# Attention output projections: three contraction pairs in the third and fourth column blocks take seven block products, not eight, in both layers

## The chip, the cores and the metric

The kernel runs on one core of one Trainium2 chip. The metric is the device time of one execution in microseconds (us). TensorE is called PE, VectorE DVE, ScalarE ACT; SP is the engine that only issues DMAs here.

## The reference, cut to what matters

A two-layer trunk, 256 tokens, 2048 columns, float32. Layer 0 mixes tokens with forgetting attention (FoX, 16 heads of 128), layer 1 with sliding-window attention (SWA, 32 heads of 64). Each mixer ends in an output projection of shape 256x2048 by 2048x2048, and then comes a gated MLP.

```
def fox_mixer(...):
    ...
    return o.reshape(b, s, FOX_QKV) @ w_out      # 2048 x 2048
def swa_mixer(...):
    ...
    return o.reshape(b, s, SWA_Q) @ w_out        # 2048 x 2048
for i in range(DEPTH):
    h = rms_norm(x, attn_norm[i]); x = x + mixer(h, ...)
    h = rms_norm(x, ffn_norm[i]);  x = x + conv_glu_ffn(h, ...)
```

## The kernel before, in words

**Numbers in two parts.** Every float32 operand of a large product is split into a high part (rounded to fp32r) and a low part (the rest). A product is three matmuls: high by high, low by high, high by low. For weights, ACT copies `raw` to `whi` and DVE subtracts to get `wlo`; both happen for every unit.

**Units.** Weights stream in units of 128 x 1024 floats (512 KB), through four slots (`RAW = 4`) of `raw`, `whi`, `wlo`. SP loads unit u when `wlo` of unit u-4 is made. In the list of steps that every engine follows in the same order, the step `("unit", u, ...)` means: PE multiplies unit u; ACT and DVE convert unit u+4 (`conv_hi`, `conv_lo`). ACT can begin that conversion only when PE has finished unit u, since the slot is the same.

**The output projection.** It has 32 units, numbered 0 to 31 here. A unit is one column block g (512 of the 2048 output columns) and two of the 16 contraction tiles (j, 0 to 7). It takes 12 matmuls of 128 x 512: 2 contraction tiles x 2 token tiles x 3. The activations are `oT` (high and low). Blocks are walked g = 0, 1, 2, 3 with all j each (FoX), or 0 and 1 interleaved, then 2, then 3 (SWA).

**The border into the MLP.** When block g is complete, DVE adds it to the residual stream `xk` (`res`, `residual`, L1052). One unit later PE transposes those columns (`xt`, L1484, 8 transposes), and ACT and DVE scale them into `hs` (`prep`, L732 and L1060, four instructions each); ACT also squares them (`ss`, L723). `transposes(n, g)` waits for `res` of its own block and, for g above 0, for `prep` of the block before:

```
pe.wait_ge(v_x, x_after(n, g))
pe.wait_ge(v_hl, KT * n + 4 * g - (4 if g == 0 else 0))
```

**The down projection of the MLP** already has units of another kind, in pairs "s" and "t". Such a pair covers two column blocks and the same contraction rows as two plain units, with seven products of blocks (Strassen-Winograd) in place of eight. For it DVE first makes sums of weight blocks (`seven_sums`, L1007, L1009, L1011, into `tsum`), ACT and DVE split the sums (`thi` L698, `tlo` L989, 128x2048), and after the last pair the products are combined into `xk` in two parts (`seven_out`, L1020 to L1031; step `ev`). The activation sums for it (`xs`) were made earlier and come back from memory.

Of the kernel before, what the change touches and what calls it, by code (L numbers as in the profile page):

```python
# [29 lines left out]
P = 128  # L30
# [75 lines left out]
PAIRS = [(layer, c, i) for layer, order in enumerate(DOWN_ORDER) for i, (kind, c, k) in enumerate(order) if kind == "s"]  # L106
# [22 lines left out]
def trunk(nc, x, attn_norm, ffn_norm, fox_w_in, fox_f_bias, fox_q_norm, fox_k_norm, fox_w_out,  # L129
# [7 lines left out]
    with ExitStack() as ctx:  # L137
# [62 lines left out]

        qT = rg("qT", [P, 4, T])
# [45 lines left out]
        nsk = rg("nsk", [P, SWA_GROUPS, 2])  # L247
        gq = sb("gq", [P, SWA_D])
# [115 lines left out]
        a_ev = sem("a_ev")  # L364
        v_e = sem("v_e")
# [26 lines left out]
        def fox_plan():  # L392
            steps = []
            for p in range(FOX_GROUPS + 1):
# [22 lines left out]
                for i in range(24 if p < FOX_GROUPS else OUT_EARLY):  # L417
                    if p < FOX_GROUPS:
                        steps += front.get(i, [])
                        steps.append(("unit", fox_unit(24 * p + i), "QKV"[i // 8], p, i % 8))  # L420
                        steps += new.get(i, [])
                    else:
                        steps.append(("unit", U_FOX_OUT + i, "o", 0, i))
                    if p == 0:
                        steps += first.get(i, [])
                    else:
                        steps += old.get(i, [])
            return steps

        def swa_plan():  # L430

            steps = []
            for slot in range(8 * SWA_CHUNKS + SWA_OUT_EARLY):
# [18 lines left out]
                if slot < 8 * SWA_CHUNKS:  # L452
                    steps.append(("unit", U_SWA + slot, "W", slot // 8, slot % 8))
                else:
                    n = slot - 8 * SWA_CHUNKS
                    steps.append(("unit", U_SWA_OUT + n, "o") + SWA_ORDER[n])
# [4 lines left out]
        def border_steps(units, n, last):  # L461

            steps, waiting = [], None
            for u, kind, g, j in units:
# [11 lines left out]
        def out_plan(base, first, n):  # L476
            order = FOX_ORDER if n == 1 else SWA_ORDER
            return border_steps([(base + i, "o") + order[i] for i in range(first, OUT_UNITS)], n, 7)
# [26 lines left out]
        def seven_kind(u):  # L505

            for m, (layer, c, i) in enumerate(PAIRS):
                if u - down_unit(layer, i) in (0, 1):
                    return "st"[u - down_unit(layer, i)], m
            return None, None  # L510

        def pairs_done(layer, c):

            return sum(p[:2] <= (layer, c) for p in PAIRS)

# [40 lines left out]
        def xt_banks(n, g):  # L556

            return (4, 6, 2, 4)[g] if n == 0 else 4
# [23 lines left out]
        def _(sp):  # L582
# [43 lines left out]
            for n in range(OUT_UNITS):  # L626
                load(U_FOX_OUT + n, rows(fox_w_out[0], 2 * (n % 8), 2, 512 * (n // 8), 512), (U_FOX_OUT + n) % RAW)

            def ffn_loads(layer):
# [14 lines left out]
                for i, (kind, g, k) in enumerate(DOWN_ORDER[layer]):  # L644
                    col = {"d": g, "s": 2 * g, "t": 2 * g + 1}[kind]
                    load(down_unit(layer, i), rows(ffn_w_down[layer], 2 * k, 2, 512 * col, 512), down_unit(layer, i) % RAW)
                    kind, m = seven_kind(down_unit(layer, i) - 2)
                    if kind == "s":
                        if first_pair(m):
                            sp.wait_ge(unit_done, down_unit(layer, 0))  # L650
                            sp.wait_ge(v_glo, UP_GROUPS * (layer + 1) + 1)
                            sp.wait_ge(x_sent, 16 * (MIX_GROUPS * (layer + 1) + 1))
                        if m >= RING:
                            sp.wait_ge(unit_done, down_unit(PAIRS[m - RING][0], PAIRS[m - RING][2]) + 2)
                        group = DOWN_ORDER[layer][PAIRS[m][2]][2] // 2
                        sp.dma_start(xs[m % RING][:, :, :, :].bitcast(F32).rearrange("p a h t -> p (a h t)"), mix[layer, group + 1, :, :])\
                            .then_inc(x_back[m % RING], 16)
# [7 lines left out]
            for n, (g, j) in enumerate(SWA_ORDER):  # L665
                load(U_SWA_OUT + n, rows(swa_w_out[0], 2 * j, 2, 512 * g, 512), (U_SWA_OUT + n) % RAW)
# [14 lines left out]
        def _(act):  # L681
# [5 lines left out]
            def conv_hi(u, slot):  # L687
# [5 lines left out]
                if kind == "t":  # L693
                    act.activation(whi[slot][:, 0:512], raw[slot][:, 0:512], ACT.Copy).then_inc(hi_ready, 1)
                    act.wait_ge(v_t, 3 * m + 3)
                    if m:
                        act.wait_ge(v_tl, m)
                    act.activation(thi[:, :, :], tsum[:, :, :], ACT.Copy).then_inc(a_th, 1)  # L698
# [10 lines left out]
            def square_x(n, g):  # L709
# [10 lines left out]
                if n == 2:  # L720
                    act.wait_ge(v_e, 7 * 2)
# [21 lines left out]
            def step(s):  # L743
# [10 lines left out]
                elif kind == "ev":  # L754
                    if s[3] == 0:
                        act.wait_ge(unit_done, s[4] + 1)
                        act.wait_ge(v_tl, pairs_done(n // 2 - 1, s[2]))
                        act.activation(tsum[:, 0, :], ps[:, 6, :], ACT.Copy).then_inc(a_ev, 1)
# [212 lines left out]
        def _(dve):  # L971
            tt = dve.tensor_tensor

            def conv_lo(u):
# [10 lines left out]
                if kind == "t":  # L985
# [3 lines left out]
                    tt(tlo[:, :, :], tsum[:, :, :], thi[:, :, :].bitcast(F32), ALU.subtract).then_inc(v_tl, 1)  # L989
# [3 lines left out]
            def seven_sums(u, m):  # L993

                layer, c, _ = PAIRS[m]
# [4 lines left out]
                if first_pair(m):  # L1000
# [3 lines left out]
                if m:  # L1004
                    dve.wait_ge(v_tl, m)
                    dve.wait_ge(v_e, 7 * (2 * layer + c))
                tt(tsum[:, 0:2, :], both[:, 1:3, :], b12, ALU.add).then_inc(v_t, 1)  # L1007
                dve.wait_ge(v_t, 3 * m + 1)
                tt(tsum[:, 2, :], tsum[:, 0, :], b22, ALU.add).then_inc(v_t, 1)  # L1009
                dve.wait_ge(v_t, 3 * m + 2)  # L1010
                tt(tsum[:, 3, :], tsum[:, 2, :], b21, ALU.add).then_inc(v_t, 1)  # L1011

            def seven_out(n, c, part, u):

                e0, q = 7 * (2 * (n // 2 - 1) + c), lambda b: ps[:, b, :]
# [24 lines left out]
            def residual(n, g, u):  # L1040
# [3 lines left out]
                if n % 2 == 0:  # L1044
                    dve.wait_ge(v_e, 7 * (2 * (n // 2 - 1) + g // 2 + 1))
# [18 lines left out]
            def step(s):  # L1064
# [266 lines left out]
        def _(pe):  # L1331
# [16 lines left out]
            def seven_unit(s):  # L1348

                _, u, kind, c, k = s  # L1350
                layer, i = (0 if u < U_SWA else 1), k // 2
                m, slot = seven_kind(u)[1], u % RAW
                first, last = i == 0, i == SEVEN[layer][c] - 1
                w = lambda buf, kj: buf[slot][:, 512 * kj:512 * kj + 512]
                sums = lambda buf, a: buf[:, a, :]
                act_in = lambda f, t: (lambda h: gs[:, i, f, h, t * P:t * P + P])
                mixed = lambda a: (lambda h: xs[m % RING][:, a, h, :])
# [8 lines left out]
                if kind == "s":  # L1366
                    if first:
                        pe.wait_ge(v_up, UP_GROUPS * (layer + 1) + 1)
                        if c:
                            pe.wait_ge(v_e, 7 * (2 * layer + c))  # L1370
                    product(4, act_in(1, 0), w(whi, 1), w(wlo, 1), first, last)
                    product(0, act_in(0, 0), w(whi, 0), w(wlo, 0), False, False).then_inc(unit_done, 1)
# [5 lines left out]
                product(5, mixed(3), sums(thi, 0), sums(tlo, 0), first, last)  # L1378
                product(7, mixed(1), sums(thi, 1), sums(tlo, 1), first, last)
                product(6, mixed(0), sums(thi, 2), sums(tlo, 2), first, last)  # L1380
                product(1, act_in(0, 1), sums(thi, 3), sums(tlo, 3), False, False).then_inc(unit_done, 1)

            def token_unit(s):
# [7 lines left out]
                opens = at == FIRST_OF[layer][g] if kind == "d" else j == 0  # L1391
# [77 lines left out]
            def transposes(n, g):  # L1469

                if n:
                    pe.wait_ge(v_x, x_after(n, g))
                    pe.wait_ge(v_hl, KT * n + 4 * g - (4 if g == 0 else 0))
                    if n == 2 and g == 0:
                        pe.wait_ge(v_up, UP_GROUPS + 1)
                        pe.wait_ge(v_e, 7 * 2)
# [223 lines left out]
```

## Time and profile before

| | |
|---|---|
| time, median of 3 runs | 2081.77 us (2080.77 to 2082.47) |
| the profiled execution: its own time | 2082.18 us |
| its span, first to last instruction | 2080.4 us |
| PE busy | 2072.3 us, 10836 matmuls |
| DVE busy | 1472.2 us |
| ACT busy | 1069.1 us |

The span is what the trace covers; about 1.8 us of the execution's time lie outside it. Matmul ends are modelled, so distances between matmuls are read from start to start. A time that an engine sat idle, and what ended it, stands in brackets at the end of a timeline row.

### The profile page before, as it was taken

How to read it: one execution, taken by the hardware profiler on the slowest of the kernel's cores; microseconds unless marked ns; L12 is line 12 of the kernel's file. 1: busy time of each engine (PE TensorE's matmuls, PEld its weight loads, DVE VectorE, ACT ScalarE, POOL GpSimd, SP SyncE). 2: the span in 40 equal slices, each digit the busy share in tenths (PEclk: the TensorE clock that was granted, in tenths of full speed). 3: DMA queues.
4: the chain of work that ended last, by engine and by line, in shares of the span. 5: the costliest groups of instructions: out<-in, count | busy, mean ns of one | idle time of the engine just before them, and what ended most of it. 6: DMA issues, size and time to landing. Idle time of an engine off the chain costs nothing.

```text
span 2080.4 us, 30179 instructions
## 1 busy us (share of the span) xinstructions
PE 2072.3 (100%) x10836; PEld 1772.4 (85%) x10836; DVE 1472.2 (71%) x1794; ACT 1069.1 (51%) x1379; POOL 0.7 (0%) x5
## 2 busy tenths in 40 slices
PE   9999999999999999999999999999999999999999
PEld 8888888888888888888888888888888888888887
DVE  5655565567767767778886687566767767778987
ACT  6545555554444544455555566554444444455553
POOL 0000000000000000000000000000000000000000
PEclk9999999999999999999999999999999999999999
DMA  7655555656666566578786544566656666668786
GB/s 251 213 172 173 168 173 179 187 174 208 195 202 204 191 200 212 192 226 258 242 254 185 181 149 139 173 189 192 193 192 220 191 196 209 200 206 260 244 258 208
DMA packets 214043, 419.02 MB, mean 201 GB/s; under 512 B 13724, under 2 KB 18636, under 8 KB 213964
## 3 DMA queue, kind: packets, MB, share of 16 engines
q1 hardware_dynamic: 211660, 415.76, 63.5%
q10 hardware_dynamic: 2304, 2.20, 0.3%
q8 instruction: 50, 0.82, 0.2%
q14 instruction: 29, 0.24, 0.0%
HBM read 405.31 MB, written 12.60 MB: 201 GB/s over the span
## 4 chain that ended last, share of the span: by engine, by line
PE 95%; DVE 3%; ACT 1%; issue 1%; DMA 1%; DVEq 0%; ACTq 0%
PE ps L1345 37%; PE ps L1335 31%; PE ps L1341 16%; PE ps L1360 2%; PE ps L1362 2%; PE ps L1361 2%; PE ps L1484 1%; DVE wlo L991 0%; DMA raw<-in_ffn_w_down 0%; PE ps L1541 0%; PE ps L1553 0%; PE ps L1570 0%; PE ps L1587 0%; PE ps L1606 0%; PE ps L1596 0%
## 5 line engine op out<-in xcount | busy, mean ns | idle before, releaser
L1335 PE MATMUL ps<-hs,whi 128*128 128x512 f32 x2832 | 663.6, 390 | 0.0
L1335 PEld LDWEIGHTS ps<-hs,whi 128*128 128x128 f32 x2832 | 524.7, 188 | 104.3
L1038 DVE TENSOR_TENSOR wlo<-raw,whi 128x1024 fp32r<-128x1024 f32 x352 | 418.1, 1222 | 254.8 <-PE ps L1341 222.8
L991 DVE TENSOR_TENSOR wlo<-raw,whi 128x1024 fp32r<-128x1024 f32 x342 | 413.7, 1222 | 215.1 <-ACT whi L700 214.6
L700 ACT ACTIVATE whi<-raw 128x1024 fp32r<-128x1024 f32 x344 | 363.2, 1059 | 341.3 <-PE ps L1345 281.0
L707 ACT ACTIVATE whi<-raw 128x1024 fp32r<-128x1024 f32 x352 | 366.0, 1056 | 265.5 <-DMA raw<-in_ffn_w_up 206.2
L1341 PEld LDWEIGHTS ps<-hs,wlo 128*128 128x128 f32 x2816 | 352.6, 191 | 8.8
L1341 PE MATMUL ps<-hs,wlo 128*128 128x256 f32 x2816 | 355.3, 283 | 0.0
L1345 PE MATMUL ps<-whi,hs 128*128 128x512 f32 x1088 | 273.9, 394 | 0.7 <-ACT whi L700 0.7
L1345 PEld LDWEIGHTS ps<-whi,hs 128*128 128x128 f32 x1088 | 201.4, 188 | 41.9 <-DVE hs L1060 0.9
L1345 PE MATMUL ps<-whi,gs 128*128 128x512 f32 x864 | 214.2, 389 | 0.0
L1345 PEld LDWEIGHTS ps<-whi,gs 128*128 128x128 f32 x864 | 161.9, 188 | 33.4
L1345 PE MATMUL ps<-wlo,hs 128*128 128x512 f32 x544 | 145.7, 389 | 0.0
L1345 PE MATMUL ps<-whi,oT 128*128 128x512 f32 x512 | 128.6, 393 | 0.6 <-DVE oT L1232 0.6
L1345 PEld LDWEIGHTS ps<-wlo,hs 128*128 128x128 f32 x544 | 102.1, 188 | 21.4
L1345 PE MATMUL ps<-wlo,gs 128*128 128x512 f32 x432 | 116.0, 389 | 0.0
L1345 PEld LDWEIGHTS ps<-whi,oT 128*128 128x128 f32 x512 | 94.8, 188 | 20.7 <-DVE oT L1232 0.8
L1345 PEld LDWEIGHTS ps<-wlo,gs 128*128 128x128 f32 x432 | 81.1, 188 | 16.8
L698 ACT ACTIVATE thi<-tsum 128x2048 fp32r<-128x2048 f32 x34 | 65.2, 1919 | 43.8 <-DVE tsum L1011 43.8
L989 DVE TENSOR_TENSOR tlo<-tsum,thi 128x2048 fp32r<-128x2048 f32 x34 | 78.0, 2293 | 8.8 <-ACT thi L698 8.8
L1277 DVE SCALAR_TENSOR_TENSOR ybuf<-gbuf,conv,ybuf 128x256 f32<-128x256 f32 x176 | 73.5, 481 | 0.0
L935 ACT ACTIVATE gs<-hf 128x1024 f32 (+1 forms) x22 | 23.3, 1061 | 91.7 <-DVE hf L1288 91.7
(190 smaller groups left out, 1558.5 us busy)
## 6 DMA issues: line engine op xcount, KB each, us to landing
raw<-in_ffn_w_up SPq DMA_DIRECT2D x352, 512.0 KB, 4.1
raw<-in_ffn_w_down SPq DMA_DIRECT2D x176, 512.0 KB, 5.4
raw<-in_fox_w_in SPq DMA_DIRECT2D x98, 512.0 KB, 4.1
raw<-in_swa_w_in SPq DMA_DIRECT2D x40, 512.0 KB, 3.7
xs<-mix SPq DMA_DIRECT2D x34, 512.0 KB, 6.4
raw<-in_fox_w_out SPq DMA_DIRECT2D x32, 512.0 KB, 4.6
raw<-in_swa_w_out SPq DMA_DIRECT2D x32, 512.0 KB, 3.9
mix<-mix_out SPq DMA_DIRECT2D x20, 512.0 KB, 6.2
```

The lines of the kernel that those rows point to most:

```text
L698: act.activation(thi[:, :, :], tsum[:, :, :], ACT.Copy).then_inc(a_th, 1)
L700: act.activation(whi[slot][:, :], raw[slot][:, :], ACT.Copy).then_inc(hi_ready, 1)
L707: act.activation(whi[u0 % RAW][:, :], raw[u0 % RAW][:, :], ACT.Copy).then_inc(hi_ready, 1)
L989: tt(tlo[:, :, :], tsum[:, :, :], thi[:, :, :].bitcast(F32), ALU.subtract).then_inc(v_tl, 1)
L991: tt(wlo[slot][:, :], raw[slot][:, :], whi[slot][:, :].bitcast(F32), ALU.subtract).then_inc(lo_ready, 1)
L1038: tt(wlo[slot][:, :], raw[slot][:, :], whi[slot][:, :].bitcast(F32), ALU.subtract).then_inc(lo_ready, 1)
L1277: last = dve.scalar_tensor_tensor(ybuf[:, f, :], gbuf[:, f, w:w + T], c(w), ybuf[:, f, :], ALU.mult, ALU.add)
L1335: return pe.matmul(ps[:, bank, :], whi[slot][:, c:c + P], moving.rearrange("p h t -> p (h t)"), start=first, stop=last)
L1341: return pe.matmul(ps[:, bank, 0:T], wlo[slot][:, c:c + P], moving[:, 0, :], start=False, stop=last)
L1345: return pe.matmul(ps[:, bank + t, :], src[:, h, t * P:(t + 1) * P], w[slot][:, 512 * kj:512 * kj + 512], start=first, stop=last)
L1360: pe.matmul(ps[:, bank, :], x(0), hi, start=start, stop=False)
L1361: pe.matmul(ps[:, bank, :], x(1), hi, start=False, stop=False)
```

## The change

In both output projections, three pairs of units of blocks 2 and 3 (j = 0, 2, 4) become pairs "s" and "t" of seven products. The other five j of these blocks stay plain. The order of the units changes: (2,1), (3,1), then s0 t0, (2,3), (3,3), s2 t2, (2,5), (3,5), s4 t4, then (2,6), (2,7), (3,6), (3,7), as (g, j). Blocks 0 and 1 stay as they are. The products use buffers of their own, `tsum_o`, `thi_o`, `tlo_o`; the activation sums are made by DVE and ACT from `oT`, in steps `xf`, `xc`, `xs` after units 5, 7 and 9. The transposes of block 1 go to another bank.

```
 def out_order(n):
...
+    plain(OUT_LEAD[n])
+    for s, j in enumerate(seven_j):
+        order.extend((("s", 1, j), ("t", 1, j)))
+        if s < OUT_SEVEN[n] - 1:
+            plain(1)
+    order.extend([("o", g, j) for g in (2, 3) for j in left])
...
+        SUMS = {1: {5: "xf", 7: "xc", 9: "xs"}, 3: {5: "xf", 7: "xc", 9: "xs"}}
...
+                u, (kind, g, j) = base + i, OUT_ORDER[n][i]
+                if i - LAST_OUT_SEVEN[n] in (1, 2):
+                    steps.append(("ev", n, 1, i - LAST_OUT_SEVEN[n] - 1, base + LAST_OUT_SEVEN[n]))
                 if j == last:
                     steps.append(("res", n, g, u))
                 steps.append(("unit", u, kind, g, j))
-                if n <= 3 and waiting is not None:
+                if waiting is not None:
                     steps += [("xt", n, waiting), ("prep", n, waiting)]
                     waiting = None
-                if n <= 3 and j == last:
+                if j == last:
                     steps.append(("ss", n, g))
                     waiting = g
+                if i in SUMS[n]:
+                    steps.append((SUMS[n][i], n))
...
         def xt_banks(n, g):
 
+            if n % 2 and g == 1:
+                return 2 if n == 1 else 0
             return (4, 6, 2, 4)[g] if n == 0 else 4
...
+                elif kind == "xs":
+                    act.wait_ge(o_xc, n // 2 + 1)
+                    act.activation(xs_o[n][:, :, :, 0, :], xc_o[n][:, :, :, :], ACT.Copy).then_inc(o_xh, 1)
...
+                elif kind == "xf":
+                    dve.wait_ge(*((v_ol, FOX_H) if n == 1 else (s_ol, 2 * OUT_SEVEN[n] - 1)))
...
+                    tt(xf_o[n][:, :, :, :], part(0), part(1), ALU.add).then_inc(o_xf, 1)
+                elif kind == "xc":
...
+                    tt(s1, a21, a22, ALU.subtract)
+                    tt(s3, a11, a21, ALU.subtract).then_inc(o_x1, 1)
...
+                    tt(n1, a11, s1, ALU.subtract).then_inc(o_x2, 1)
...
+                    tt(s4, a12, n1, ALU.subtract).then_inc(o_xc, 1)
+                elif kind == "xs":
+                    dve.wait_ge(o_xh, n // 2 + 1)
+                    tt(xs_o[n][:, :, :, 1, :], xc_o[n][:, :, :, :], xs_o[n][:, :, :, 0, :].bitcast(F32), ALU.subtract).then_inc(o_xs, 1)
...
-                pe.wait_ge(x_back[m % RING], 16 * (m // RING + 1))
-                product(2, mixed(2), w(whi, 0), w(wlo, 0), False, False)
+                if n % 2:
+                    pe.wait_ge(o_xs, n // 2 + 1)
+                else:
+                    pe.wait_ge(x_back[RING_NO[m] % RING], 16 * (RING_NO[m] // RING + 1))
+                product(c2, mixed(2), w(whi, 0), w(wlo, 0), False, False)
```

**DVE where blocks 0 and 1 of SWA end (units 14, 15, 16).** L1052 is `res`, L991 `conv_lo`, L1060 `prep`. Before:

```order
L1052 TENSOR_TENSOR xk<-xk,ps 128x2x512 [waits unit_done]
L991 TENSOR_TENSOR wlo_55<-raw,whi_51 128x1024 [waits hi_ready]
L1052 TENSOR_TENSOR xk<-xk,ps 128x2x512 [waits unit_done]
L991 TENSOR_TENSOR wlo_56<-raw,whi_52 128x1024 [waits hi_ready]
L1060 SCALAR_TENSOR_TENSOR hs<-ps,gains,hs 128x256 [waits a_hh]
```

In the changed kernel L1131 is `res`, L1085 to L1089 make the weight sums, L1066 and L1061 are `conv_lo`, L1064 is the low part of the sums, L1139 is `prep`:

```order
L1131 TENSOR_TENSOR xk<-xk,ps 128x2x512 [waits unit_done]
L1085 TENSOR_TENSOR tsum_o<-raw 128x1024 [waits s_ol,v_tl,w_land1,v_e,w_land0,hi_ready]
L1087 TENSOR_TENSOR tsum_o<-tsum_o,raw 128x512 [waits v_t]
L1089 TENSOR_TENSOR tsum_o<-tsum_o,raw 128x512 [waits v_t]
L1066 TENSOR_TENSOR wlo_55<-raw,whi_51 128x1024
L1131 TENSOR_TENSOR xk<-xk,ps 128x2x512 [waits unit_done]
L1061 TENSOR_TENSOR wlo_56<-raw,whi_52 128x512 [waits hi_ready]
L1064 TENSOR_TENSOR tlo_o<-tsum_o,thi_o 128x2048 [waits a_th]
L1139 SCALAR_TENSOR_TENSOR hs<-ps,gains,hs 128x256 [waits a_hh]
```

Three sums now stand between the two residual additions, and the low part of the sums between the second one and `prep` of block 0. In FoX the same instructions stand around `res` of block 1 (there `prep` of block 0 is long done).

**DVE behind the last pair (units 27 to 30), the same in both layers.** Before, `res` of block 2 stood behind unit 23, with plain conversions on both sides:

```order
L991 TENSOR_TENSOR wlo_55<-raw,whi_51 128x1024 [waits hi_ready]
L1052 TENSOR_TENSOR xk<-xk,ps 128x2x512 [waits unit_done]
L991 TENSOR_TENSOR wlo_56<-raw,whi_52 128x1024 [waits hi_ready]
L991 TENSOR_TENSOR wlo_57<-raw,whi_53 128x1024 [waits hi_ready]
L1060 SCALAR_TENSOR_TENSOR hs<-ps,gains,hs 128x256 [waits a_hh]
```

In the changed kernel (L1099 to L1110 combine the products):

```order
L1066 TENSOR_TENSOR wlo_56<-raw,whi_52 128x1024 [waits hi_ready]
L1099 TENSOR_TENSOR tsum_o<-tsum_o,ps 128x512 [waits a_ev,unit_done]
L1100 TENSOR_TENSOR xk<-xk,ps 128x512
L1102 TENSOR_TENSOR tsum_o<-tsum_o,ps 128x512 [waits v_e]
L1103 TENSOR_TENSOR xk<-xk,ps 128x512
L1066 TENSOR_TENSOR wlo_57<-raw,whi_53 128x1024 [waits hi_ready]
L1106 TENSOR_TENSOR xk<-xk,tsum_o 128x2x512 [waits v_e]
L1108 TENSOR_TENSOR xk<-xk,tsum_o 128x512 [waits v_e]
L1110 TENSOR_TENSOR xk<-xk,ps 128x512 [waits v_e]
L1131 TENSOR_TENSOR xk<-xk,ps 128x2x512 [waits unit_done,v_e]
```

The residual addition of block 2 now stands behind all seven combining instructions. PE's transposes of block 2 still come after one further unit, now unit 30, and wait for it.

## Rows read from the trace of the kernel before

**Rows 1.** The page: busy us by engine; granted PE clock in 40 slices.

```profile
PE 2072.3 (100%) x10836; PEld 1772.4 (85%) x10836; DVE 1472.2 (71%) x1794; ACT 1069.1 (51%) x1379; POOL 0.7 (0%) x5
...
PEclk9999999999999999999999999999999999999999
```

**Rows 2.** Who waited for whom, PE: us in total, times, longest us.

```profile
PE ps L1664 <- DVE ones_t L1302: 1.2, 1, 1.2
PE ps L1360 <- DVE tlo L989: 1.0, 2, 0.8
```

**Rows 3.** Timeline: two plain units following each other (start us, us, instruction).

```profile
1350.16 1.98 PE L1345 MATMUL ps<-whi,oT 128*128 128x512 f32 x8
...
1352.88 1.98 PE L1345 MATMUL ps<-whi,oT 128*128 128x512 f32 x8
```

**Rows 4.** Timeline, down projection: a plain unit behind each of two pairs.

```profile
1033.92 1.98 PE L1345 MATMUL ps<-whi,gs 128*128 128x512 f32 x8
...
1044.12 1.98 PE L1345 MATMUL ps<-whi,gs 128*128 128x512 f32 x8
```

**Rows 5.** Groups by line: busy us, mean ns of one, idle before.

```profile
L991 DVE TENSOR_TENSOR wlo<-raw,whi 128x1024 fp32r<-128x1024 f32 x342 | 413.7, 1222 | 215.1 <-ACT whi L700 214.6
L700 ACT ACTIVATE whi<-raw 128x1024 fp32r<-128x1024 f32 x344 | 363.2, 1059 | 341.3 <-PE ps L1345 281.0 <-DMA raw<-in_ffn_w_down 44.4 <-PE ps L1362 9.8
L989 DVE TENSOR_TENSOR tlo<-tsum,thi 128x2048 fp32r<-128x2048 f32 x34 | 78.0, 2293 | 8.8 <-ACT thi L698 8.8
L698 ACT ACTIVATE thi<-tsum 128x2048 fp32r<-128x2048 f32 x34 | 65.2, 1919 | 43.8 <-DVE tsum L1011 43.8
L1011 DVE TENSOR_TENSOR tsum<-tsum,raw 128x512 f32<-128x512 f32 x34 | 23.5, 693 | 1.2
L1206 DVE TENSOR_TENSOR oT<-ps,oT 128x256 fp32r<-128x256 f32 x16 | 6.0, 416 | 0.0
```

**Rows 6.** Timeline, FoX, units 14 to 16.

```profile
355.41 1.23 DVE L991 TENSOR_TENSOR wlo<-raw,whi 128x1024 fp32r<-128x1024 f32 x1 [1.50 <-ACT whi L700]
...
356.98 1.22 DVE L1052 TENSOR_TENSOR xk<-xk,ps 128x1024 f32<-128x1024 f32 x1 [0.34 <-PE ps L1345]
...
359.51 1.03 PE L1484 MATMUL ps<-ident,xk 128*128 128x128 f32 x8
```

**Rows 7.** Timeline, SWA, units 14 to 16.

```profile
1310.01 1.23 DVE L991 TENSOR_TENSOR wlo<-raw,whi 128x1024 fp32r<-128x1024 f32 x1
...
1312.18 2.09 PE L1345 MATMUL ps<-whi,oT 128*128 128x512 f32 x8
...
1313.88 1.65 DVE L1060 SCALAR_TENSOR_TENSOR hs<-ps,gains,hs 128x256 fp32r<-128x256 f32 x4
...
1315.68 1.06 PE L1484 MATMUL ps<-ident,xk 128*128 128x128 f32 x8 [0.49 <-DVE hs L1060]
```

**Rows 8.** Timeline, down projection of layer 0: behind the last pair.

```profile
1084.92 1.98 PE L1345 MATMUL ps<-whi,gs 128*128 128x512 f32 x8
...
1093.51 1.07 PE L1484 MATMUL ps<-ident,xk 128*128 128x128 f32 x8 [0.27 <-DVE xk L1031]
```

**Rows 9.** Timeline, SWA: the last attention groups, beside units 7 to 11.

```profile
1285.37 1.23 DVE L991 TENSOR_TENSOR wlo<-raw,whi 128x1024 fp32r<-128x1024 f32 x1 [0.75 <-ACT whi L700]
...
1289.24 1.22 DVE L1215 TENSOR_REDUCE mxs<-ps 128x8 f32<-128x1024 f32 x1
...
1295.55 0.69 DVE L1229 TENSOR_TENSOR prs<-prs,rls 128x512 f32<-128x512 f32 x1
...
1298.35 1.04 PE L1596 MATMUL ps<-ident,prs 128*128 128x128 f32 x8
```

**Rows 10.** Issues of loads: KB each, median us from issue to landing.

```profile
raw<-in_swa_w_out SPq DMA_DIRECT2D x32, 512.0 KB, 3.9
```

**Rows 11.** Timeline: the first matmuls of the kernel, and the same shape later.

```profile
1.19 4.92 PE L1664 MATMUL ps<-ones_t 128*128 128x128 f32 x22 [1.19 <-DVE ones_t L1302]
...
7.41 1.06 PE L1672 MATMUL ps<-ones_t 128*128 128x128 f32 x8
```

More of the change, by code:

```diff
@@ L247, in trunk @@
         nsk = rg("nsk", [P, SWA_GROUPS, 2])
+        assert inr[0] <= xs_at
         gq = sb("gq", [P, SWA_D])
@@ L422, in fox_plan @@
                     else:
-                        steps.append(("unit", U_FOX_OUT + i, "o", 0, i))
+                        steps.append(("unit", U_FOX_OUT + i) + OUT_ORDER[1][i])
                     if p == 0:
@@ L459, in swa_plan, with out_plan @@
             return steps
-        def border_steps(units, n, last):
-            steps, waiting = [], None
-            for u, kind, g, j in units:
+        def out_plan(base, first, n):
+            steps, waiting, last = [], None, 7
+            for i in range(first, OUT_UNITS):
+                u, (kind, g, j) = base + i, OUT_ORDER[n][i]
+                if i - LAST_OUT_SEVEN[n] in (1, 2):
+                    steps.append(("ev", n, 1, i - LAST_OUT_SEVEN[n] - 1, base + LAST_OUT_SEVEN[n]))
                 if j == last:
@@ L505, in seven_kind, with seven_buffers, seven_banks, evicted @@
         def seven_kind(u):
-            for m, (layer, c, i) in enumerate(PAIRS):
-                if u - down_unit(layer, i) in (0, 1):
-                    return "st"[u - down_unit(layer, i)], m
+            for m, p in enumerate(PAIRS):
+                if u - p[2] in (0, 1):
+                    return "st"[u - p[2]], m
             return None, None
-        def pairs_done(layer, c):
-            return sum(p[:2] <= (layer, c) for p in PAIRS)
+        def seven_buffers(n):
+            return (tsum_o, thi_o, tlo_o) if n % 2 else (tsum, thi, tlo)
+        def seven_banks(n):
+            return {1: (0, 6, 4, 5, 2, 3), 3: (2, 6, 4, 5, 0, 1)}.get(n, (0, 2, 4, 5, 6, 7))
+        def evicted(n, c):
+            return 7 * STAGES.index((n, c))
+        def pairs_done(n, c):
+            return sum(p[:2] <= (n, c) for p in PAIRS)
         def first_pair(m):
@@ L697, in conv_hi @@
                         act.wait_ge(v_tl, m)
-                    act.activation(thi[:, :, :], tsum[:, :, :], ACT.Copy).then_inc(a_th, 1)
+                    act.activation(high[:, :, :], sums[:, :, :], ACT.Copy).then_inc(a_th, 1)
                     return
@@ L988, in conv_lo @@
                     dve.wait_ge(a_th, m + 1)
-                    tt(tlo[:, :, :], tsum[:, :, :], thi[:, :, :].bitcast(F32), ALU.subtract).then_inc(v_tl, 1)
+                    sums, high, low = seven_buffers(PAIRS[m][0])
+                    tt(low[:, :, :], sums[:, :, :], high[:, :, :].bitcast(F32), ALU.subtract).then_inc(v_tl, 1)
                     return
@@ L1366, in seven_unit @@
                 if kind == "s":
-                    if first:
+                    if first and n % 2:
+                        pe.wait_ge(v_hl, KT * n + 4)
+                    elif first:
                         pe.wait_ge(v_up, UP_GROUPS * (layer + 1) + 1)
                         if c:
-                            pe.wait_ge(v_e, 7 * (2 * layer + c))
-                    product(4, act_in(1, 0), w(whi, 1), w(wlo, 1), first, last)
-                    product(0, act_in(0, 0), w(whi, 0), w(wlo, 0), False, False).then_inc(unit_done, 1)
+                            pe.wait_ge(v_e, evicted(n, c))
+                    product(q1, act_in(1, 0), w(whi, 1), w(wlo, 1), first, last)
+                    product(c1, act_in(0, 0), w(whi, 0), w(wlo, 0), False, False).then_inc(unit_done, 1)
                     return
-                pe.wait_ge(x_back[m % RING], 16 * (m // RING + 1))
-                product(2, mixed(2), w(whi, 0), w(wlo, 0), False, False)
+                if n % 2:
+                    pe.wait_ge(o_xs, n // 2 + 1)
+                else:
+                    pe.wait_ge(x_back[RING_NO[m] % RING], 16 * (RING_NO[m] // RING + 1))
+                product(c2, mixed(2), w(whi, 0), w(wlo, 0), False, False)
                 pe.wait_ge(a_th, m + 1)
                 pe.wait_ge(v_tl, m + 1)
[L1378 to L1381, printed above, removed]
+                product(q5, mixed(3), sums(high, 0), sums(low, 0), first, last)
+                if first and n % 2:
+                    pe.wait_ge(v_hl, KT * n + 8)
+                product(q7, mixed(1), sums(high, 1), sums(low, 1), first, last)
+                product(q6, mixed(0), sums(high, 2), sums(low, 2), first, last)
+                product(c1 + 1, act_in(0, 1), sums(high, 3), sums(low, 3), False, False).then_inc(unit_done, 1)
             def token_unit(s):
```

130 lines of the change are left out of this document (88 added, 42 removed).

## The prediction

> **What bounds the kernel now.** I read the page first: PE is busy for 2072.3 of the 2080.4 us of the span, and its clock row shows nine tenths or more in every slice [rows 1]. Then the waits of PE: beyond the start there are none over 0.8 us [rows 2]. So the kernel is a stream of matmuls, and what I look for is how many matmuls go, and where PE will wait for DVE or ACT, which have had room until now. A plain unit takes 2.72 us from start to start, 0.227 us for each of its 12 matmuls [rows 3]. The rest of the reading was timelines of PE, DVE and ACT around the four places where the edit puts work: the end of attention in SWA, the border between blocks 1 and 2 in each layer, and the stretch behind the last pair in each layer. I followed the three engines' orders there, with durations from the rows.
>
> **What goes.** A pair has 21 matmuls where two plain units have 24. Three pairs in two layers take away 6 x 3 = 18 matmuls, all on the path: 18 x 0.227 = **-4.1 us**. That pairs run at the full rate of PE is seen in the down projection: a plain unit, a plain unit and a pair, 45 matmuls, take 10.20 us, 0.227 each [rows 4]. DVE has some 9.3 us to do in that time (two sums of 512, one of 1024, one `tlo`, three conversions and a half one: 2 x 0.69 + 1.22 + 2.29 + 3 x 1.22 + 0.69 [rows 5]), so it keeps up, barely. The Trainium skill, "TensorE: Matmul & The Clock Gate", section "Back-to-back issue gap", gives N/2.4 + 2.5 ns, 216 ns for 512 columns; by that figure the saving would be 3.9 us and the sum 0.2 us higher. The trace has 227 ns, and I take that.
>
> **What comes, first place: the border of blocks 0, 1 and 2 in FoX, +1.0 us.** The conversion of unit 18 (the first "s") happens at unit 14 and now has three sums ahead of it, 1.22 + 0.69 + 0.69 = 2.6 us [rows 5]. It began at 355.41; its `wlo` will then start at 358.0 and end at 359.2. Behind it in DVE's queue stands `res` of block 1, 1.2 us, so it ends at 360.4 and not at 358.2. PE's transposes of block 1, which began at 359.51 [rows 6], follow it by 0.15 us (the distance between `prep`'s end at 1313.88 + 1.65 and 1315.68 in [rows 7]): 360.5. PE waits 1.0 us. Next in the queue are `tlo` (to 363) and `prep` of block 1 (to 366.0); PE needs them at the second and third product of t0, 366.1 and 366.7. That fits, with 0.7 us to spare for the later one. Bounds: 0.5 (the sums overlap more) to 1.5 (that spare fails).
>
> **Second place: the same border in SWA, +3.9 us.** Here `prep` of block 0 comes behind the pair's work too. From 1310.01 [rows 7], as before but with sums: `wlo` of unit 18 ends at 1313.8, `res` of block 1 at 1315.0, the half conversion of unit 19 at 1315.7, `tlo` (2.29) at 1317.9, `prep` of block 0 (1.65) at 1319.5. ACT isn't the later one: `thi` can start at 1312.7 and ends at 1314.6, its half of `prep` at 1316.2. The transposes of block 1 wait for `prep` of block 0 (the second wait in `transposes`): they start at 1319.6, not at 1315.68. That is +3.9 us. PE could have started them at 1315.0 (1312.18 + 2.72, and 0.1 more for a unit that follows transposes: 2.09 there, 1.98 in [rows 3]), so it already lost 0.65 there. Behind that, `prep` of block 1 ends near 1322.6, and t0 needs it at 1325.8: covered. Bounds: 3.0 (all DVE steps overlap by 0.15 us) to 4.5.
>
> **Third place: the end of attention in SWA, +0.8 us.** Steps xf, xc and xs are new, and no row has their shapes. xf and the second half of xs have 1536 elements per partition: between 1.22 us (1024) and 2.29 (2048), 1.76 by line. ACT's copy of 1536 lies between 1.06 and 1.92: 1.49. xc is four operations of 384, between 0.42 and 0.69 each: 0.55, together 2.2 [rows 5]. xf stands ahead of a maximum of scores, and so delays ACT's exponentials and the conversion of unit 11 behind them by 1.7 less the idle 0.75: it ends at 1287.5. xc makes it 1289.7, the next conversion 1290.8, and the next maximum starts there and not at 1289.24 [rows 9]. ACT's exponentials follow 1.5 us late, then ACT's copy of xs puts 1.4 more ahead of the last group's, and DVE's half of xs 0.3 more ahead of its normalisation: `prs`, which ended at 1295.55 + 0.69 = 1296.2, ends at 1299.4. Its four transposes are the second half of the eight from 1298.35 [rows 9], due at 1298.75; they start at 1299.55. PE waits 0.8 us. With the smaller neighbours (1024, 256) it is 0; with the larger ones (2048, 512) 2.2. In FoX the same steps stand beside plain units, where DVE idles 1.5 us in each (the bracket in [rows 6]): nothing, and if that cover were gone, the 0.8 of here.
>
> **Fourth place: behind the last pair, +1.75 us in each layer.** The down projection shows this stretch: from the first unit behind the last pair, at 1084.92, to the transposes that waited for the last combining instruction, at 1093.51, are 8.59 us; three units are 8.16, so it cost only 0.27 there [rows 8]. In the projections `res` of block 2 stands between the last combining instruction and the transposes: +1.22 us. They can start 9.8 us after the last pair, where PE is ready at 8.16: a wait of 1.65. ACT's squares of block 2, `prep` of block 2 and `res` of block 3 shift with it; I get 0.1 us more at the transposes of block 3. Before, the transposes of block 2 had no such wait. Together **+3.5 us**. Bounds for each: 0.3 (as the down projection) to 2.3.
>
> **Loads.** SP's loads wait for `wlo` of four units earlier, so a late DVE issues them late. At the worst, behind the second place, unit 24 is loaded from 1320.6 and needed at 1330; a landing takes 3.9 us [rows 10]. Hidden. Without that cover it would be the excess over 9 us.
>
> **Sum**: -4.1 + 1.0 + 3.9 + 0.8 + 3.5 = **+5.1 us**. The profiled execution's own time is 2082.18, of which 2080.4 are the span; that is 0.4 above the median of the three runs. On the median, 2081.77 + 5.1 = **2086.9 us**, 0.25% slower. All low bounds give -4.1 + 0.5 + 3.0 + 0 + 0.6 = 0.0, all high ones +8.7.
>
> **The rivals.** (a) The waits don't come: DVE is busy for 71% only [rows 1], and 34 pairs in the down projections cost PE 1.0 us of waits in all [rows 2]. Then the 18 matmuls are the whole effect: 2077.7, faster by 0.2%. It decides if DVE is ahead by more than 4 us at 1310 and 2 us behind the last pairs; against it, `res` of blocks 0 and 2 can't start before PE's unit is done, so no lead can be stored up. (b) Only the end is shorter: the transposes of block 2 wait 0.3 us as in [rows 8]. Then 2086.9 - 2 x 1.4 = 2084.1. Against it stands the order, with `res` behind the last combining instruction. (c) The pairs don't catch up behind a late first one: DVE has 0.9 us of room in 10.2, and the second pair of the down projection waited 0.8 us [rows 2]. Once in each layer: +1.6, 2088.5. For it speaks the small room, against it that the second pair has 5.4 us of plain units ahead. (d) The clock. In SWA PE would stand still for 4.6 us before the transposes of block 1, longer than any wait of the trace. After its idle start, 22 matmuls of 128 columns took 4.92 us, 0.21 each; the same shape later takes 0.11 [rows 11], though the clock row shows no fall. Should PE restart like that, it would run at half its pace for some 5 us and lose 2.5: 2089.4. The Trainium skill, "TensorE: Matmul & The Clock Gate", section "Why this matters for your kernels", says that a long idle gap between bursts of matmuls brings PE back to half its clock; by that rule (d) is what happens, and the trace has no gap that tests it.
>
> **How the numbers follow.** 0.2% is 4.2 us, about what a measurement of this kernel can tell from no change. My forecast has a chance of 0.55, with its own range 2085.5 to 2088.3; 0.07 of it is below 2085.9, so within 0.2%. (a) 0.08, half of it faster by over 0.2%. (b) 0.12, within. (c) 0.10 and (d) 0.15, slower. Slower: 0.48 + 0.10 + 0.15 = 0.73; same: 0.07 + 0.04 + 0.12 = 0.23; faster: 0.04. The range 2083.5 to 2089.8 leaves out (a), the worse half of (d) and the edges of (b), under 0.2 together.
>
> **What would show it.** In the changed profile PE has 18 matmuls less, 10818. The waits of PE have the transposes of `xk` at the top: one of some 4.6 us in SWA, one of 1.0 in FoX, two of 1.6 behind the last pairs, and one of 0.8 before the last transposes of `prs`. DVE is busier by some 50 us. If the transposes' waits sum to less than 4 us, the queue argument is wrong; if matmuls of 512 columns behind the 4.6 us gap are spaced 0.45 us, (d) holds.

## The result, and the profile after

The changed kernel takes **2089.26 us** (median of 7 runs, 2088.25 to 2089.75), the kernel before 2081.60 on the same chip: ratio 1.0035, 95% interval 1.0025 to 1.0045, slower. All four places of the forecast came within 0.3 us of their size, and the clock, which I had kept as rival (d), came on top. The page, as in [rows 1]:

```profile
PE 2071.6 (99%) x10818; PEld 1770.9 (85%) x10818; DVE 1515.2 (73%) x1844; ACT 1081.0 (52%) x1389; POOL 0.7 (0%) x5
...
PEclk9999999999999999999999999999999999999999
```

18 matmuls are gone, yet PE is busy for only 0.7 us less, not 4.1: others must have become longer. The clock row can't show it, since a slice of it is 52 us long. PE's waits (us in total, times, longest), against [rows 2]:

```profile
PE ps L1590 <- DVE hs L1139: 4.3, 1, 4.3
PE ps L1590 <- DVE xk L1131: 3.6, 3, 1.4
...
PE ps L1459 <- DVE tlo L1064: 0.8, 1, 0.8
...
PE ps L1702 <- DVE prs L1325: 0.4, 1, 0.4
```

L1590 is the transposes: one wait for `prep`, three for `res`. The timeline of SWA around the long one, against [rows 7]:

```profile
1313.59 2.09 PE L1441 MATMUL ps<-whi,oT 128*128 128x512 f32 x8
1314.02 1.22 DVE L1066 TENSOR_TENSOR wlo<-raw,whi 128x1024 fp32r<-128x1024 f32 x1
...
1315.15 1.22 DVE L1131 TENSOR_TENSOR xk<-xk,ps 128x1024 f32<-128x1024 f32 x1
...
1316.89 2.29 DVE L1064 TENSOR_TENSOR tlo_o<-tsum_o,thi_o 128x2048 fp32r<-128x2048 f32 x1
...
1319.09 1.65 DVE L1139 SCALAR_TENSOR_TENSOR hs<-ps,gains,hs 128x256 fp32r<-128x256 f32 x4
...
1320.89 1.94 PE L1590 MATMUL ps<-ident,xk 128*128 128x128 f32 x8 [4.29 <-DVE hs L1139]
...
1322.48 3.76 PE L1441 MATMUL ps<-whi,oT 128*128 128x512 f32 x8
...
1326.04 1.30 PE L1441 MATMUL ps<-wlo,oT 128*128 128x512 f32 x4
1327.18 0.40 PE L1459 MATMUL ps<-whi,oT 128*128 128x512 f32 x1
```

Unit 16 starts at 1313.59; 12 matmuls behind transposes take 2.83 us at full speed, so PE is ready at 1316.42 and starts at 1320.89: 4.5 us later, where it was 0.67 in [rows 7]. Then look at the length of what follows. The eight transposes take 1.59 us from start to start (0.82 before), unit 17 takes 4.70 (2.85 before, from 1316.50 to 1319.35); its first eight matmuls are spaced 0.445 us. The windows of the same stretch say why. The columns are the window, its length, the busy times of PE, PEld (PE's loading of weights), DVE, ACT and POOL with the number of instructions, the granted PE clock, the share of time in which the DMA engines were busy, and GB/s:

```profile
1310.00:1315.00 5.00, 5.00 (x28) 4.22 (x27) 4.66 (x5) 3.89 (x7) 0.00 (x0) 1.00 0.34 105
1315.00:1320.00 5.00, 1.60 (x7) 0.95 (x6) 5.00 (x7) 4.67 (x10) 0.00 (x0) 0.97 0.57 172
1320.00:1322.00 2.00, 1.11 (x6) 1.14 (x7) 1.87 (x3) 0.00 (x0) 0.00 (x0) 0.50 0.25 95
1322.00:1325.00 3.00, 3.00 (x10) 2.52 (x9) 1.73 (x4) 1.68 (x4) 0.00 (x0) 0.50 0.56 166
1325.00:1327.00 2.00, 2.00 (x7) 1.52 (x7) 0.00 (x0) 0.00 (x0) 0.00 (x0) 0.63 0.04 13
1327.00:1332.00 5.00, 5.00 (x24) 4.10 (x23) 3.24 (x4) 2.12 (x2) 0.00 (x0) 1.00 0.19 46
```

The granted clock is 0.50, which is 1.2 and not 2.4 GHz. It fell while PE still stood (0.97 over 1315 to 1320, and PE starts at 1320.89), and it rose again between 1325 and 1327. Price: 0.77 for the transposes and 1.85 for unit 17, 2.6 us.

FoX, the border of blocks 1 and 2, against [rows 6]:

```profile
355.33 1.23 DVE L1085 TENSOR_TENSOR tsum_o<-raw 128x1024 f32<-128x1024 f32 x1 [1.49 <-ACT whi L771]
...
359.06 1.22 DVE L1131 TENSOR_TENSOR xk<-xk,ps 128x1024 f32<-128x1024 f32 x1
...
360.33 0.88 PE L1590 MATMUL ps<-ident,xk 128*128 128x128 f32 x6 [0.75 <-DVE xk L1131]
```

The transposes stood at 359.51 before, in a timeline that ran 0.08 later there: +0.9 us. The end of attention in SWA, against [rows 9]:

```profile
1278.41 1.75 DVE L1155 TENSOR_TENSOR xf_o<-oT 128x1536 f32<-128x1536 f32 x1
...
1288.13 0.55 DVE L1160 TENSOR_TENSOR xc_o<-xf_o 128x384 f32<-128x384 f32 x1
...
1295.17 1.49 ACT L832 ACTIVATE xs_o<-xc_o 128x1536 fp32r<-128x1536 f32 x1
...
1299.14 0.60 PE L1702 MATMUL ps<-ident,prs 128*128 128x128 f32 x4
...
1299.38 0.69 DVE L1325 TENSOR_TENSOR prs<-prs,rls 128x512 f32<-128x512 f32 x1
...
1300.12 0.55 PE L1702 MATMUL ps<-ident,prs 128*128 128x128 f32 x3 [0.39 <-DVE prs L1325]
```

The prices read off the line through [rows 5] (1.76, 1.49, 0.55) hold to 0.01 us. The second four transposes were due 0.4 us behind the first, at 1299.54, and start at 1300.12: +0.6. Behind the last pair of FoX, against [rows 8]:

```profile
394.62 1.98 PE L1441 MATMUL ps<-whi,oT 128*128 128x512 f32 x8
...
396.94 0.68 DVE L1110 TENSOR_TENSOR xk<-xk,ps 128x512 f32<-128x512 f32 x1
397.65 1.22 DVE L1131 TENSOR_TENSOR xk<-xk,ps 128x1024 f32<-128x1024 f32 x1
...
398.93 1.09 PE L1590 MATMUL ps<-ident,xk 128*128 128x128 f32 x8 [1.43 <-DVE xk L1131]
```

PE is ready at 394.62 + 2.72 = 397.34 and starts at 398.93: +1.6, and in SWA the same (1362.12, also with 1.43 in brackets). The sum is -4.1 + 0.9 + 3.8 + 0.6 + 3.2 + 2.6 = **+7.0 us**, and the spans differ by 2087.5 - 2080.4 = 7.1; the medians by 7.7.

### The profile page after: what moved, and what is told of

The parts are those of the page before. It is cut to its first block, busy times and chain, and to the rows that moved or that the text cites. A ratio compares the mean times of both kernels' runs of the same rounds, so it can differ in the third digit from the quotient of the medians.

```text
span 2087.5 us, 30253 instructions
## 1 busy us (share of the span) xinstructions
PE 2071.6 (99%) x10818; PEld 1770.9 (85%) x10818; DVE 1515.2 (73%) x1844; ACT 1081.0 (52%) x1389; POOL 0.7 (0%) x5
## 4 chain that ended last, share of the span: by engine, by line
PE 94%; DVE 4%; ACT 1%; issue 1%; DMA 0%; DVEq 0%; ACTq 0%
PE ps L1441 35%; PE ps L1431 31%; PE ps L1437 16%; PE ps L1459 3%; PE ps L1461 3%; PE ps L1460 3%; PE ps L1590 1%; DVE wlo L1066 1%; ACT whi L771 1%; PE ps L1647 0%; PE ps L1659 0%; PE ps L1676 0%; ACT prs L964 0%; PE ps L1667 0%; DMA grow<-in_attn_norm 0%
## 5 line engine op out<-in xcount | busy, mean ns | idle before, releaser
L1066 DVE TENSOR_TENSOR wlo<-raw,whi 128x1024 fp32r<-128x1024 f32 x336 | 405.7, 1222 | 177.2 <-ACT whi L771 176.6
L1441 PE MATMUL ps<-whi,oT 128*128 128x512 f32 x416 | 106.6, 399 | 0.6 <-DVE oT L1328 0.6
L1441 PEld LDWEIGHTS ps<-whi,oT 128*128 128x128 f32 x416 | 77.8, 191 | 17.3 <-DVE oT L1328 0.8
L1064 DVE TENSOR_TENSOR tlo<-tsum,thi 128x2048 fp32r<-128x2048 f32 x34 | 77.9, 2293 | 8.5 <-ACT thi L769 8.5
```

The lines of the kernel that those rows point to most:

```text
L1064: tt(low[:, :, :], sums[:, :, :], high[:, :, :].bitcast(F32), ALU.subtract).then_inc(v_tl, 1)
L1066: tt(wlo[slot][:, :], raw[slot][:, :], whi[slot][:, :].bitcast(F32), ALU.subtract).then_inc(lo_ready, 1)
L1441: return pe.matmul(ps[:, bank + t, :], src[:, h, t * P:(t + 1) * P], w[slot][:, 512 * kj:512 * kj + 512], start=first, stop=last)
```

## The experiments

The kernel before had a median of 2081.51 us beside fill, fox_only, swa_only and prep_first, 2081.37 beside gap2, gap3, tail_order and xs_later, and 2081.40 beside tail_bank and repaired. Differences below are against these.

### fill: matmuls in the standstill

The changed kernel, and ahead of the transposes of block 1 in SWA:

```
...
+for _ in range(16):
+    pe.matmul(ps[:, 6, :], oT[:, 0, 0, 0:P], oT[:, 0, :, :].rearrange("p h t -> p (h t)"), start=True, stop=True)
```

> The changed kernel with 16 matmuls of 128x512 that nobody reads, put into PE's queue ahead of the transposes of block 1 in SWA, where PE stands still for 4.5 us (it was idle for 4.3 by the list of waits); they need 3.6 us. Theory (the clock): PE's granted clock falls to 0.5 behind the idle stretch, and the 8 transposes and the next unit take 2.7 us longer for that (6.29 us from the first transpose to the next unit's successor, where before they took 3.6). With the stretch filled, the clock stays at 1.00, the transposes take 0.8 us again, and the kernel is 2.7 us faster than the changed one: +4.6 us over before, 0.22%. Rival (contention: transposes and matmuls are slow there because ACT and DVE read the same banks or memory): filling changes nothing, +7.3 us, 0.35%. A second rival: the filling delays the transposes themselves, more than 0.35%.

Measured: 2085.83 us, ratio 1.0021 (1.0012 to 1.0030). The transposes stand where they stood, but the clock doesn't fall; timeline of PE:

```profile
1315.63 3.79 PE L1621 MATMUL ps<-oT 128*128 128x512 f32 x16
1320.12 1.06 PE L1590 MATMUL ps<-ident,xk 128*128 128x128 f32 x8 [0.70 <-DVE hs L1139]
1320.94 2.09 PE L1441 MATMUL ps<-whi,oT 128*128 128x512 f32 x8
1322.87 1.07 PE L1441 MATMUL ps<-wlo,oT 128*128 128x512 f32 x4
```

Transposes 0.82, unit 17 in 2.83 us: full speed, in the same place and with the same work of DVE, ACT and the DMAs beside it. This takes contention out as the cause. The median fell by 3.4 us, not 2.7. The profiled spans differ by 3.5: 2.6 for the clock, and 0.8 for a wait for `tlo` in a down projection, which the changed kernel's profile has and this one hasn't. Whether that wait belongs to the kernel or to the one execution that was profiled is not known.

### fox_only and swa_only: one layer at a time

```
-OUT_SEVEN = {1: 3, 3: 3}
+OUT_SEVEN = {1: 3, 3: 0}      # fox_only; {1: 0, 3: 3} in swa_only
...
```

The rest of the edit takes the other layer's steps, buffers and bank back to what they were.

> Seven-product pairs in the FoX output projection only; the SWA one is as before. Theory by the ledger of waits: 9 matmuls less (-2.0), 0.9 at the transposes of block 1, 1.65 behind the last pair, 0.1 at the transposes of block 3: +0.5 us, 0.02 to 0.04% over before, no difference that can be told. Rival (the pairs themselves cost something that the list of waits does not show): more than +2 us, 0.1%.

Measured: 2082.16 us, +0.65, ratio 1.0002 (0.9993 to 1.0011). The interval reaches +2.3 us, so it leaves little of the rival, but not nothing.

> Seven-product pairs in the SWA output projection only; the FoX one is as before. Theory: -2.0 + 0.75 (end of attention) + 3.8 (transposes of block 1) + 2.7 (clock) + 1.7 (behind the last pair) = +6.9 us, 0.33% over before, nearly the whole loss. Rival (the two layers share the loss): +3.6 us, 0.17%.

Measured: 2088.36 us, +6.9, ratio 1.0027 (1.0017 to 1.0037). The two parts add up to 7.5, the whole is 7.7. That swa_only hits its forecast to 0.1 us is in part luck: its nine runs fall into groups, four at 2086.0 to 2086.6, four at 2088.4 to 2088.6 and one at 2090.5, and the median is the lowest of the second. Why they do was not tried. In FoX, where PE never stands still for over 1.6 us, the pairs about pay for their waits (-2.05 + 0.9 + 1.6 = +0.5 by the terms). Nearly all of the loss is SWA's.

### prep_first: the order of DVE's queue in SWA

```
 if kind == "unit":
-    if n + RAW < U_END:
+    if n + RAW < U_END and n != U_SWA_OUT + 15:
         conv_lo(n + RAW)
...
 elif kind == "prep":
     prep(n, s[2])
+    if (n, s[2]) == (3, 0):
+        conv_lo(U_SWA_OUT + 19)
```

and the same for ACT with `conv_hi`.

> The changed kernel, with one edit in SWA: ACT and DVE convert unit 19 (the half conversion and the split of the weight sums, 0.7 + 2.3 us on DVE) behind prep of block 0 and not ahead of it. Theory: prep of block 0 ends 3 us earlier, the transposes of block 1 start with a wait of 1.5 us, not 4.5, and the clock does not fall: -2.9 - 2.7 = -5.6 us against the changed kernel, +1.7 over before, 0.08%. The first t then needs the split sums 5.6 us after the transposes start; they come 2.7 us after. Rival 1 (prep of block 0 is not what the transposes wait for): no gain, 0.35%. Rival 2 (the wait only moves to the first t): +4 us, 0.2%.

Measured: 2083.30 us, +1.8, ratio 1.0006 (0.9997 to 1.0015). Its waits of PE:

```profile
PE ps L1594 <- DVE xk L1133: 3.6, 3, 1.4
PE ps L1594 <- DVE hs L1141: 1.5, 1, 1.5
```

The `hs` wait fell from 4.3 to 1.5, the granted clock's mean is 1.000, and 5.9 us of the 7.7 are gone by the place of one conversion in the queue. `prep` standing behind `tlo` was the cause of the standstill, and the standstill of the clock's fall.

### gap2 and gap3: a standstill without any pair

The kernel before, with k additions (2 in gap2, 3 in gap3) of 128x1024 on DVE, whose result nobody reads, ahead of `prep` of block 0 in SWA:

```
+for m in range(k):
...
+    tt(t1[:, :, :, :], t2[:, :, :, :], t2[:, :, :, :], ALU.add)
...
 prep(n, s[2])
```

> The kernel before (no pair in the projections), with two additions of 128x1024 by DVE that nobody reads, 1.25 us each, between the conversion of unit 19 and prep of block 0 in SWA. Both theories: the transposes of block 1 start 2.5 us later. PE stands still for some 3.1 us before them. If a standstill of that length keeps the clock, the kernel is 2.5 us over before (0.12%); if it lowers it, the transposes take 1.6 us and not 0.8, and the sum is +5 us (0.24%). Contention by the pairs cannot play a part, there are none.

> As the last, with three additions: the transposes of block 1 start 3.75 us later, and PE stands still for some 4.4 us, as in the changed kernel. Theory (the standstill alone lowers the clock): 3.75 + 2.7 = +6.4 us over before, 0.31%, with the granted clock at 0.5 behind the transposes. Rival (the slow stretch belongs to the pairs, by contention): +3.75 us, 0.18%, clock 1.00.

Measured: gap2 2085.22 us, +3.85, ratio 1.0017 (1.0008 to 1.0026); gap3 2087.62 us, +6.25, ratio 1.0031 (1.0019 to 1.0043). Timeline of gap3, then of gap2:

```profile
1317.79 1.94 PE L1492 MATMUL ps<-ident,xk 128*128 128x128 f32 x8 [4.15 <-DVE hs L1061]
1319.38 3.76 PE L1353 MATMUL ps<-whi,oT 128*128 128x512 f32 x8
...
1322.94 1.20 PE L1353 MATMUL ps<-wlo,oT 128*128 128x512 f32 x4
1323.98 1.31 PE L1353 MATMUL ps<-whi,oT 128*128 128x512 f32 x5
```

```profile
1317.90 1.51 PE L1492 MATMUL ps<-ident,xk 128*128 128x128 f32 x8 [2.89 <-DVE hs L1061]
...
1319.07 3.35 PE L1353 MATMUL ps<-whi,oT 128*128 128x512 f32 x8
...
1323.18 1.98 PE L1353 MATMUL ps<-whi,oT 128*128 128x512 f32 x8
```

gap3: the same slow stretch as in the changed kernel (1.59 and 4.60 us where 0.82 and 2.85 are due), so the idle time alone does it. Its sum is 3.6 for the longer wait and 2.5 for the clock, 6.1 of the 6.25 measured. The profiled spans differ by only 4.8 us, because this execution was 1.55 us ahead of the one before when it came to the edit (block 0's transposes at 1309.84, not 1311.39). gap2 I had expected to fall to one side; it fell to both. Its profiled execution lost 1.17 - 0.82 + 4.11 - 2.85 = 1.6 us to the clock behind 2.89 us of idle time; and of its ten runs three have a mean granted clock of 1.000 and take 2083.03 to 2083.77 (+1.7 to +2.4, the longer wait alone), seven have 0.998 or 0.999 and take 2084.58 to 2087.12. At that length the same program sometimes loses the clock and sometimes not.

### tail_order: alternating the last plain units

```
-order.extend([("o", g, j) for g in (2, 3) for j in left])
+order.extend([("o", g, j) for j in left for g in (2, 3)])
```

> The changed kernel, with the four plain units behind the last pair in the order (2,6), (3,6), (2,7), (3,7) and not (2,6), (2,7), (3,6), (3,7), in both layers; the same matmuls. The transposes of block 2 then come behind four units (10.9 us after the last pair) and not behind three (8.2 us), and the residual addition of block 2 ends 9.8 us after it. Theory: the two waits of 1.4 us (1.65 from start to start) go, and nothing takes their place: -3.3 us against the changed kernel, +4.0 over before, 0.19%. Rival (the wait moves to the transposes of block 3, which now have one MLP unit less of distance from block 2's scaling): a gain under 1 us, 0.3%.

Measured: 2088.08 us, +6.7, ratio 1.0033 (1.0021 to 1.0046). A miss: of 3.3 us I got about 1. The transposes of block 2 wait no more, but PE's waits read

```profile
PE ps L1590 <- DVE hs L1139: 6.9, 3, 4.3
...
PE ps L1590 <- DVE xk L1131: 0.8, 1, 0.8
```

and the timeline has the two new ones at the transposes of block 3, here that of SWA:

```profile
1367.07 1.06 PE L1590 MATMUL ps<-ident,xk 128*128 128x128 f32 x8 [1.29 <-DVE hs L1139]
```

They wait for `prep` of block 2, the second wait of `transposes`, for the sake of the bank that both use.

### tail_bank: and the transposes of block 3 in a bank of their own

tail_order's edit, and:

```
 def xt_banks(n, g):
+    if n % 2 and g == 3:
+        return 6
...
-pe.wait_ge(v_hl, KT * n + 4 * g - (4 if g == 0 else 0))
+pe.wait_ge(v_hl, KT * n + 4 * g - (4 if g == 0 or (n % 2 and g == 3) else 0))
```

> The changed kernel with the last plain units in the order (2,6), (3,6), (2,7), (3,7), as before in tail_order, and in addition the transposes of block 3 go to bank 6, so that they need not wait for prep of block 2. Theory: the second wait of the transposes was all that was left of the loss at the end of each layer; res of block 3 ends 1.5 us before PE is ready for these transposes, so they start without a wait, and both layers together win 3.0 us over tail_order: 2085.1 us, 0.18% over the kernel before. No wait of PE for hs is left but the 4.3 us one in SWA; xk keeps about 0.8 in FoX. Rival: DVE is behind as a whole at the end of the layer, and the wait moves once more, to the first matmuls of the MLP that read hs: 2088, 0.32%.

Measured: 2085.71 us, +4.3, ratio 1.0020 (1.0011 to 1.0029): 3.4 us less than the changed kernel, 3.0 expected over tail_order and 2.4 found. Timeline of PE in FoX:

```profile
400.15 1.04 PE L1592 MATMUL ps<-ident,xk 128*128 128x128 f32 x8
...
403.82 1.04 PE L1592 MATMUL ps<-ident,xk 128*128 128x128 f32 x8
```

Neither row has a bracket. The loss at the end of the layers was two dependences, one behind the other; removing the first only showed the second.

### xs_later: xs after unit 10 in SWA

```
-SUMS = {1: {5: "xf", 7: "xc", 9: "xs"}, 3: {5: "xf", 7: "xc", 9: "xs"}}
+SUMS = {1: {5: "xf", 7: "xc", 9: "xs"}, 3: {5: "xf", 7: "xc", 10: "xs"}}
```

> The changed kernel, with step xs of SWA (ACT's copy 1.49 us, DVE's subtraction 1.76 us) after unit 10 and not after unit 9, so behind the last group's exponentials. Theory: the last group's probabilities come 1.8 us or more earlier, the wait of 0.4 us (0.75 from start to start) at its transposes goes: -0.7 us, 0.32% over before. Rival (ACT's copy now holds up the copies of the transposed probabilities, and PE waits at the last products of attention): no gain or a small loss, 0.35 to 0.4%.

Measured: 2087.05 us, +5.7, ratio 1.0028 (1.0017 to 1.0040). The wait for `prs` is no longer among PE's waits, as expected. The median fell by 2.0 us rather than 0.7, and the profiled span by 3.1. In the profiles, 0.8 of that is again the `tlo` wait of the down projection, absent here, and 1.0 is the clock:

```profile
1318.87 1.74 PE L1590 MATMUL ps<-ident,xk 128*128 128x128 f32 x8 [4.29 <-DVE hs L1139]
1320.26 3.13 PE L1441 MATMUL ps<-whi,oT 128*128 128x512 f32 x8
```

PE stood still for the same 4.29 us as in the changed kernel, but the transposes take 1.39 us and unit 17 takes 3.88, to 1324.14: the price is 0.57 + 1.03 = 1.6 us, not 2.6. The granted clock is 1.00 until 1319, when PE has started again, and back at 1.00 from 1323. With 0.6 for `prs` that is 2.4 of the 3.1; the other 0.7 I can't place.

### repaired: all of them together

> The changed kernel with every wait treated for which an edit was found: in SWA the half conversion of unit 19 stands behind prep of block 0 (as in prep_first), xs comes after unit 10 (as in xs_later), and the last plain units and the bank of the transposes of block 3 are as in tail_bank. The FoX border stays as it is. Theory: the parts add up. From the changed kernel's 7.9 us over the kernel before: -6.0 (prep_first, with the clock), -0.7 (the wait for prs), -3.9 (the ends of the two layers) leave -2.7 us: about 2078.7 us, 0.13% under the kernel before, with the 18 matmuls less still paying 4.1. Rival: the parts don't add, since a PE that waits less leaves DVE less room and the wait moves behind the next dependence: 2082 us or more, no gain over the kernel before.

Measured: 2079.81 us, -1.6, ratio 0.9992 (0.9983 to 1.0001). PE's waits:

```profile
PE ps L1596 <- DVE hs L1143: 1.5, 1, 1.5
PE ps L1465 <- DVE tlo L1068: 1.5, 2, 0.8
...
PE ps L1596 <- DVE xk L1135: 0.8, 1, 0.8
```

The parts nearly add up: 9.3 us under the changed kernel, where 10.6 were forecast (0.7 of the difference is one more wait for `tlo` in a down projection). Against the kernel before the interval just touches 1, so no gain is shown; what can be said is that the loss is gone. Of the 4.1 us that the matmuls pay, the two remaining borders take back 0.9 (FoX) and 1.0 (SWA: 1.67 from start to start, less the 0.67 that PE lost there before), and the `tlo` wait, 1.5 against 1.0 before, 0.5 in the profiled execution. That leaves 1.7.

## Why the prediction was right, and where it was off

Right in sign, with the time inside the range, 2.4 us above the forecast, and that is rival (d). The forecast's own range, 2085.5 to 2088.3, was missed: the time lies inside the stated range because that took in part of (d). So the queue argument was right, and the clock stood outside it.

- **What goes** (-4.1): 10818 matmuls, as forecast. fox_only's median is within 0.2 us of its terms, which rest on this price, with an interval of 1.9 us to each side.
- **First place** (+1.0): 0.9, and `res` at 359.06 (359.2 forecast). That there was spare for `tlo` and `prep` of block 1 held too: no wait for `tlo_o` stands in the list.
- **Second place** (+3.9): 3.8. prep_first and gap3 show its cause from both sides.
- **Third place** (+0.8): 0.6; xs_later removes it.
- **Fourth place** (+3.5): 3.2. The 1.65 per layer were 1.6. The prediction gives the down projection's cost as 0.27 us, which is idle time; from start to start it is 8.59 - 8.16 = 0.43, the figure that its 1.65 uses, and (b) and the low bound should have had it too. The 0.1 more at the transposes of block 3 didn't come, but tail_order shows that their wait stood right behind.
- **DVE** busier by 43 us, not 50.
- **(a)** and **(b)** are refuted by the waits. **(c)**: pairs catch up; no wait for `tlo_o` stands in the list, and the wait for `tlo` in the down projections is 0.8, 1.0 before. That wait varies from profile to profile, absent in fill, 1.5 in repaired, 2.1 in swa_only, though no edit is near it; with one profile of each kernel, whether it goes with the kernel or the execution stays open.
- **(d)**: the failed step. I wrote that it would cost 2.5 us and space matmuls by 0.45, and it was 2.6 and 0.445. The time that it gave, 2089.4, is the one measured (2089.26), in part by luck: the waits were 0.7 us smaller than in the sum, and the medians lie 0.6 further apart than the profiled spans. But I gave it 0.15, because "the trace has no gap that tests it". That was true, and the wrong way to weigh it: the forecast itself had PE stand still for 4.6 us, over three times any wait of the trace, and [rows 11] showed matmuls at half their pace at the one place where PE came from standing still, the start. That was evidence for (d), and none stood against it but the clock row. The row is too coarse to show a few microseconds, and at the start it can't show them at all: windows of 1 us read 1.00 there too, but the clock record in the packed trace begins only 5.84 us into the span. In repaired it begins at 4.16 us and the first 22 matmuls take 4.12 us; in prep_first at 6.45, and they take 5.06. It belonged in the sum, not among the rivals. The Trainium skill, "TensorE: Matmul & The Clock Gate", section "Why this matters for your kernels", states that a long idle gap brings PE back to half its clock; the trace agrees (idle 4.29 us, granted clock 0.50 behind it).

## What to carry to other kernels

When an edit puts work on a helper engine, follow that engine's queue to the next instruction that the busy engine waits for: here 18 matmuls less earned 4.1 us, and work placed ahead of `res`, `prep` and `prs` in DVE's queue took back 8.5. A long standstill costs more than its length: behind 2.9 us the clock fell in seven runs of ten here, and behind 4.15 us or more in every profile, so add the slow stretch behind it, 1.6 to 2.6 us. And before spending an experiment on removing a wait, write down the next wait of the same instruction, since it may stand a few tenths behind.

## What the runs showed of the hardware that I had not expected

The clock fell behind idle times of 4.29 us (changed kernel, tail_order, tail_bank, xs_later), 4.32 (swa_only), 4.15 (gap3) and, in seven of ten runs, behind one that was 2.89 us in the profiled run (gap2). Behind 1.49 us (prep_first, repaired) and 1.43 us (twice in the changed kernel) it did not fall; between 1.5 and 2.89 us nothing was measured.

The length of the standstill doesn't fix the price. It was 2.5 to 2.6 us in five of these profiles, but 1.6 in xs_later, whose standstill was as long as the changed kernel's, and 1.6 in gap2. In the dear cases the clock fell while PE still stood (changed kernel: 0.97 over 1315 to 1320, start at 1320.89; gap3: 0.72 over 1315 to 1318, start at 1317.79). In the two cheap ones it fell only after PE had started again (gap2: 1.00 over 1315 to 1318, 0.69 in the next microsecond, start at 1317.90). What sets the moment stays open. A price that varies so within one standstill may be part of the spread of the runs, but the spread alone doesn't tell: gap2's ten runs spread over 4.1 us, and so do fill's eleven, with a mean granted clock of 1.000 in each.

Sixteen matmuls whose result nobody reads were worth about 2.6 us, by keeping PE busy in a wait that it had anyway.
